# Modulation rows from natural weight rows on VectorE, most of them made during later stages

## The reference

```python
c_act = jax.nn.silu(c)
for layer in range(DEPTH):                                  # 2
    mod = c_act @ ada_w[layer] + ada_b[layer]               # 1024 x 6144, 24 MB a layer
    sh1, sc1, g1, sh2, sc2, g2 = jnp.split(mod, 6, axis=-1)
    h = modulate(rmsnorm(x, norm_mix[layer]), sh1, sc1)     # h * (1 + sc) + sh
    y = retention_mixer(...) if layer == 0 else sgu_mixer(...)
    x = x + g1 * y
    h = modulate(rmsnorm(x, norm_ffn[layer]), sh2, sc2)
    x = x + g2 * peer_ffn(h, ...)                           # 128 experts per token
```

## Time and profile before

| | us |
|---|---|
| median of three runs | 2549.06 |
| profiled execution | 2548.47 |
| its span, first to last instruction | 2546.6 |
| PE busy | 2118.2 (83%) |
| VectorE busy | 1592.1 (63%) |
| ScalarE busy | 1092.5 (43%) |
| POOL busy | 592.9 (23%) |
| DMA | 763.12 MB, 300 GB/s over the span |

### The profile page before, as it was taken

The page is one execution under the profiler, slowest core; times in us unless marked ns, Lnnn a source line. Parts: engine busy times, 40 slices in busy tenths (PEclk is TensorE's granted clock), DMA queues, the critical chain, the costliest instruction groups (busy, mean ns, idle before and its releaser), DMA issues. The chain is left out here.

```text
span 2546.6 us, 24726 instructions
## 1 busy us (share of the span) xinstructions
PE 2118.2 (83%) x8508; PEld 1354.2 (53%) x8508; DVE 1592.1 (63%) x2934; ACT 1092.5 (43%) x2137; POOL 592.9 (23%) x547
## 2 busy tenths in 40 slices
PE   6789997978877878859978787888887887978998
PEld 5669866532222222237967553443332226867996
DVE  6777455776667666534774767767676654555553
ACT  5554433444443444324433444344444343434442
POOL 0000001444444434300000344444344430300000
PEclk9999998999999999979998998999999998889999
DMA  8876535999999999945535899999999994323553
GB/s 310 301 283 234 193 115 178 418 419 421 421 422 421 421 421 422 421 129 179 177 106 173 324 417 376 420 418 419 412 418 421 421 419 130 118 91 116 165 183 132
DMA packets 195327, 763.12 MB, mean 300 GB/s; under 512 B 24545, under 2 KB 26625, under 8 KB 128769
## 3 DMA queue, kind: packets, MB, share of 16 engines
q0 software_dynamic: 75216, 545.88, 51.8%
q1 hardware_dynamic: 105218, 207.75, 23.9%
q10 hardware_dynamic: 14768, 7.92, 1.1%
HBM read 760.41 MB, written 1.10 MB: 299 GB/s over the span
## 5 line engine op out<-in xcount | busy, mean ns | idle before, releaser
L651 PE MATMUL pair<-uv,p_diag 128*128 128x512 f32 x1360 | 668.3, 626 | 160.0 <-ACT p_diag L1623 155.8
L916 DVE TENSOR_TENSOR ring_low<-ring,ring_high 128x2048 fp32r<-128x2048 f32 x196 | 446.1, 2289 | 272.5 <-ACT ring_high L1489 268.4
L1167 DVE CUSTOM_DVE_ANT_0 uv<-uv,p_h 128x1024 f32<-128x1024 f32 x340 | 416.3, 1224 | 302.3 <-DMA uv<-in_peer_uv,p_idx 298.3
L413 POOL DMA_INDIRECT uv<-in_peer_uv,p_idx x340 | 377.5, 1110 | 878.0 <-PE pair L651 466.7
L651 PEld LDWEIGHTS pair<-uv,p_diag 128*128 128x128 f32 x1360 | 245.7, 194 | 559.1 <-ACT p_diag L1623 321.1
L1489 ACT ACTIVATE ring_high<-ring 128x2048 fp32r<-128x2048 f32 x196 | 372.6, 1911 | 321.0 <-DMA ring<-in_ada_w 69.9
L1617 ACT ACTIVATE p_act<-p_dot 128x1 f32<-128x1 f32 x512 | 103.0, 201 | 622.5 <-DVE p_dot L1167 620.9
L522 PE MATMUL pair<-hT_high,ring_high 128*128 128x256 f32 x1056 | 309.5, 293 | 4.6 <-DVE hT_low L926 3.8
L522 PE MATMUL pair<-hT_low,ring_high 128*128 128x256 f32 x1056 | 303.6, 288 | 0.0
L522 PE MATMUL pair<-hT_high,ring_low 128*128 128x256 f32 x1056 | 303.4, 287 | 0.0
L651 PE MATMUL pair<-uv_high,p_diag 128*128 128x512 f32 x464 | 230.9, 630 | 49.8 <-ACT p_diag L1623 48.5
(11 more groups left out here) (312 smaller groups left out, 2739.1 us busy)
## 6 DMA issues: line engine op xcount, KB each, us to landing
ring<-in_ada_w SPq DMA_DIRECT2D x48, 1024.0 KB, 5.2
ring<-in_ret_w_in SPq DMA_DIRECT2D x24, 1024.0 KB, 5.1
ring<-in_sgu_w_in SPq DMA_DIRECT2D x24, 1024.0 KB, 5.2
ring<-in_peer_w_query SPq DMA_DIRECT2D x16, 1024.0 KB, 5.0
ring<-in_w_up SPq DMA_DIRECT2D x16, 1024.0 KB, 5.4
ring<-in_w_down SPq DMA_DIRECT2D x16, 1024.0 KB, 5.1
ring<-in_sgu_w_out SPq DMA_DIRECT2D x12, 1024.0 KB, 5.1
ring<-in_w_in SPq DMA_DIRECT2D x12, 1024.0 KB, 5.1
```

What stands on the lines that cost most here:

```text
L413: nc.gpsimd.indirect_dma_start(uv_rows[SLOT[l][s]].rearrange("p a d -> p (a d)"), None, experts, bass.IndirectOffsetOnAxis(ap=p_idx[:, k:k ...
L651: mm = nc.tensor.matmul(acc[:, half, :], p_diag[:, n % DIAGS, :], v[:, half * 512:(half + 1) * 512], start=(k == 0), stop=(k == PICKS - 1))
L916: did(V.tensor_tensor(ring_low[:, i % R], ring[:, i % R], ring_high[:, high_at[i]].bitcast(F32), ALU.subtract), w_low, i + 1)
L1167: V.tensor_tensor_reduce(out=u, in0=u, in1=p_h[:, s // PICKS, :], scale=1.0, scalar=0.0, op0=ALU.mult, op1=ALU.add, accum_out=p_dot[:, n % ...
```

## The change

The twelve rows are made another way. A tile of `ada_w` is now 128 rows by 1024 columns of one row's part, 0.5 MB in runs of 4 KB. VectorE adds it, scaled by silu(c) of that partition, to the tile before; after eight tiles the sum over partitions is left, and PE takes it with two fp32 products by a matrix of ones, which also spreads it over all partitions. The first tile is added to a tile of zeros that has the bias in partition 0. Scale rows are then completed by VectorE with (1 + row) x gain (`scale_row`), the others are copied by ScalarE (`take_mod`).

Rows are numbered in the order of `MODS`. Rows 0 and 1 are made at the start from sixteen buffers loaded by SyncE. Rows 2 to 7 are made during retention, rows 8 to 11 during the gating mixer; their tiles are loaded by POOL. `STAGED` gives the buffers: four for rows 2 to 6, three for row 7 and for rows 8 to 11. A tile is loaded once the addition after its buffer's last tile is done, or, where that tile was the last of its row, once PE has summed the row. `lows_and_adas(first, counts)` puts so many additions behind each low half.

The first norm and the retention product follow the first two rows; the 48 blocks of `ada_w` leave the ring. The constants by feature are packed on the host in one array `cols` loaded at the start; the other constants go from ScalarE's queue to POOL's. The position weights come turned from the host, and their sum is made by PE within the experts of layer 0. The keys of layer 0 are loaded at the end of retention.

```diff
+MODS = [(0, 1), (0, 0), (1, 0), (1, 1), (0, 2), (0, 3), (0, 4), (0, 5), (1, 2), (1, 3), (1, 4), (1, 5)]
+STAGED = ([[("arena", 8192 + 1024 * i) for i in range(8)], [("arena", 16384 + 1024 * i) for i in range(6)] + [("arena", 2048), ("arena", 3072)]]
+          + 5 * [[("arena", 20480), ("arena", 21504), ("mod", 4), ("mod", 5)]] + [[("arena", 20480), ("arena", 21504), ("mod", 5)]]
+          + 4 * [[("arena", 22528), ("arena", 23552), ("mod", 5)]])
...
+    for v, allowed in enumerate(STAGED):
+        free = [a for a in sorted(allowed, key=lambda a: held.get(a, -1))]
+        for k in range(KD):
+            place.append(free[k % len(free)])
+            before.append(held.get(place[-1]))
+            held[place[-1]] = v * KD + k
...
+        def load_ada(eng, j):
+            (l, part), k, old = MODS[j // KD], j % KD, ADA_BEFORE[j]
+            if old is not None and old % KD == KD - 1:
+                eng.wait_ge(small_ready, SMALL[("mod", old // KD, 1)] + 1)
+            elif old is not None:
+                eng.wait_ge(ada_used, old + 2)
+            eng.dma_start(ada_rows[ADA_AT[j]], w["ada_w"][l, k * P:(k + 1) * P, part * D:(part + 1) * D]).then_inc(ada_landed[j][0], 16)
...
+            sp.dma_start(col[:], w["cols"]).then_inc(c_in, 16)
+            for j in range(KD):
+                load_ada(sp, j)
+            sp.dma_start(x[:], w["x"][0].rearrange("(t p) d -> p t d", p=P)).then_inc(x_in, 16)
+            for j in range(KD, 2 * KD):
+                load_ada(sp, j)
...
+            load_gain_and_bias(0)
+            load_gain_and_bias(1)
+            modulation_rows(range(2, 8))
             gathers(0)
+            pool.wait_ge(x_ready, NORM[2] + 1)
...
+            modulation_rows(range(8, 12))
...
+            def sum_mod(v):
+                pe.wait_ge(ada_used, (v + 1) * KD)
+                rows = ada_rows[ADA_AT[(v + 1) * KD - 1]]
+                for half in range(2):
+                    name = ("mod", v, half)
+                    open_small(name)
+                    nc.tensor.matmul(small_of(name)[:, :], ones[:], rows[:, half * 512:(half + 1) * 512],
+                                     start=True, stop=True).then_inc(small_ready, 1)
...
                 for c in range(4, 12):
+                    if c in (6, 8, 10):
+                        sum_mod(c // 2 - 1)
                     rows_product(("ret_in", c), ("ret_in",), c, hT, KD)
+                sum_mod(5)
...
-                rows_product(("ret_out", 1), ("ret_out",), 1, r_ygT, 16)
+                rows_product(("ret_out", 1), ("ret_out",), 1, r_ygT, 16, lambda kb: sum_mod(6 + kb // 2) if kb % 2 == 0 else None)
...
                 for c in range(6):
+                    if c == 4:
+                        sum_mod(8)
                     rows_product(("sgu_v", c), ("sgu_v",), 6 + c, hT, KD, parts_of_hT(2))
...
+                sum_mod(9)
                 for c in range(6):
+                    if c == 3:
+                        sum_mod(10)
                     columns_product(("sgu_u", c), ("sgu_u",), c, hT)
...
+                    if kb == 1:
+                        sum_mod(11)
...
+            def adas(count):
+                for j in range(ada_done[0], ada_done[0] + count):
+                    v, k = divmod(j, KD)
+                    rows = ada_rows[ADA_AT[j]]
+                    dve.wait_ge(*ada_landed[j])
+                    if k == 0:
+                        dve.wait_ge(bias_in, 16 * (v + 1))
+                    if j:
+                        dve.wait_ge(ada_used, j)
+                    did(V.scalar_tensor_tensor(out=rows, in0=rows, scalar=col[:, k:k + 1], in1=ada_rows[ADA_AT[j - 1]] if k else bias_row,
+                                               op0=ALU.mult, op1=ALU.add), ada_used, j + 1)
...
+            def lows_and_adas(first, counts):
+                for n, count in enumerate(counts):
+                    lows(first + n)
+                    adas(count)
...
+                    if c == 8:
+                        scale_row(3)
+                    lows_and_adas(2 * c + 2, (0, 0) if c == 0 else (1, 1) if c < 4 else (2, 2))
...
+                lows_and_adas(first + 1, (2, 2, 2, 2, 2))
...
-                    lows(block_after(("sgu_v",), 6 + c))
+                    lows_and_adas(first_block_of[("sgu_v", 6 + c)] + 2, (1, 2) if c else (2, 2))
...
-                act.dma_start(s_ws, w["sgu_w_s"][0].rearrange("g i j -> i g j")).then_inc(sgu_in, 16)
-                act.dma_start(s_vbias, bc(w["sgu_b_in"][0:1, HALF:2 * HALF], [P, HALF])).then_inc(sgu_in, 16)
-                act.dma_start(s_bs.rearrange("p g i -> p (g i)"), bc(w["sgu_b_s"].rearrange("a g i -> a (g i)"), [P, GROUPS * P])).then_inc(sgu_in, 16)
...
```

More of the change, by code:

```diff
@@ L68, in matrices @@
 def matrices(w):
-    out = [(("ada", l), w["ada_w"][l], 8, range(12)) for l in range(2)]
-    out += [(("ret_in",), w["ret_w_in"][0], 8, range(12)), (("ret_out",), w["ret_w_out"][0], 16, range(2)),
+    out = [(("ret_in",), w["ret_w_in"][0], 8, range(12)), (("ret_out",), w["ret_w_out"][0], 16, range(2)),
             (("query", 0), w["peer_w_query"][0], 8, range(4)),
@@ L130, in turned, with mods @@
         return [("hT", n, t, g) for t in range(TT) for g in range(2)]
-    out = turned(0) + [("ret_s", h) for h in range(RET_HEADS)] + [("ygT", b) for b in range(8)]
+    def mods(*vs):
+        return [("mod", v, half) for v in vs for half in range(2)]
+    out = mods(0, 1) + turned(0) + mods(2, 3, 4, 5) + [("ret_s", h) for h in range(RET_HEADS)] + [("ygT", b) for b in range(8)] + mods(6, 7)
     for l in range(2):
@@ L137, in small_in_order @@
         if l == 0:
-            out += turned(2) + [("wsT", b) for b in range(2)] + [("ws_sum", b) for b in range(2)]
-            out += [("mixed", b) for b in range(CU // 2)]
+            out += [("ws_sum", b) for b in range(2)] + turned(2) + mods(8, 9, 10)
+            out += [("mixed", b) for b in range(6)] + mods(11) + [("mixed", b) for b in range(6, CU // 2)]
     out += turned(5) + [("attT", 0)]
@@ L639, in peer @@
                     t, h = divmod(i, PEER_HEADS)
+                    if l == 0 and i == WS_UNIT:
+                        pe.wait_ge(ws_zero, 1)
+                        for b in range(2):
+                            name = ("ws_sum", b)
+                            open_small(name)
+                            nc.tensor.matmul(small_of(name)[:, :], ones[:], s_wsT[:, 4 * b:4 * b + 4, :].rearrange("p g i -> p (g i)"),
+                                             start=True, stop=True).then_inc(small_ready, 1)
                     name = ("peer", l, t)
@@ L873, in mlp @@
                     rows_product(("down", c), ("down",), c, f_a, 32, lambda kb: pe.wait_ge(a_low, kb + 1))
[L876 to L892 removed]
             pe.wait_ge(ones_ready, 2)
+            sum_mod(0)
+            sum_mod(1)
+            pe.wait_ge(cst_in, 16)
+            turn_rows(0, r_h)
             retention()
@@ L954, in norm @@
                 settle()
+                if shift_mod is not None:
+                    wait_mod(dve, shift_mod)
                 for t in range(TT):
@@ L1185, in peer @@
                 for i in range(UNITS):
+                    if l == 0 and i == WS_UNIT - 1:
+                        dve.wait_ge(ws_in, 16)
+                        did(V.memset(s_wsT[CHUNK:P, :, 0:CHUNK], 0.0), ws_zero, 1)
                     for k in range(TOPK):
@@ L1251, in sgu @@
                 settle()
[L1252 removed]
+                lows_and_adas(first_block_of[("sgu_u", 2)] + 2, (1, 1))
                 for t in range(TT):
@@ L1524, in columns, with take_mod @@
                 return t.rearrange("p (a b) t -> p a (b t)", b=2)
+            def take_mod(v):
+                for half in range(2):
+                    name = ("mod", v, half)
+                    take_small(name, mod_of(v)[:, half * 512:(half + 1) * 512], small_of(name)[:, :])
             def retention():
-                load_keys(0)
                 for c in range(4):
@@ L1604, in peer @@
                 for i in range(UNITS):
+                    if l == 0 and i == WS_UNIT + 1:
+                        for b in range(2):
+                            take_small(("ws_sum", b), s_wsum[:, 4 * b:4 * b + 4, :].rearrange("p g i -> p (g i)"), small_of(("ws_sum", b))[:, :])
                     if l == 1 and i in (5, 7, 9, 11):
```

293 lines of the change are left out of this document (133 added, 160 removed).

## The result

The changed kernel takes 2473.4 us (median of 4 runs, 2469.2 to 2477.3) against 2550.2 for the kernel before, measured beside it: ratio 0.970, 95% interval 0.967 to 0.973, so 76.8 us less. I had said 2464, in a range from 2425 to 2500.

A forecast was written before the change was run, and what follows sets the result against it. PE bounds retention and gating products, DMA the first stage and experts. Terms -141.3 + 22.5 + 12 + 18.6 + 1.3 + 7.9 - 5.4 = -84.4 took 2548.5 to 2464 us; 8-in-10 range 2425 to 2500, own range 2440 to 2480.

The forecast's parts named there:

- Start: Before retention: only two rows remain to be made, so PE starts at 47 us, -141.3 us.
- Retention product: Retention product: four row sums 6.9, three stops 10, clock 4.2 and 1.4, together +22.5 us.
- Heads: Behind the retention product: head 0's scores wait for row 5's sum, a tile landing and additions, +12 us.
- Output product with what follows: Output product of retention: additions ahead of lows, a 9.6 us stop, row 7's sum and clock, +18.6 us.
- Experts and third norm's reciprocal: Layer 0 experts +1.3 us; the third norm's reciprocal no longer waits for ScalarE's DMA issues, -18.1 us.
- Gating stage behind it: Gating stage: additions, sums and clock 33.3 us on; reciprocal and weight detour 25.4 off, +7.9 in all.
- One sign of the list: First gating product: chunks of 12 to 14 us would show the forecast right.
- Later norms: Later norms: reciprocals find the root 2.3 and 3.1 us sooner, -5.4 us.
- Rival (a): All stages with additions: tiles arrive early wherever VectorE asks, so waits are hidden; 2401 us, chance 0.13.
- Rival (b): Tile loads: landing of 6 us as ring and POOL share, 12 in retention, 10 in gating; 2486 us, chance 0.20.
- Rival (c): All exposed waits: landings beyond 9.3 us make the kernel slower than before, about 2670 at 15.8; chance 0.03.
- the 2443 us worked out from the page: Some 13 exposed landings: by the skill page's 3.2 us each would be 1.6 shorter, giving about 2443 us.

The follow-up runs named there:

- more buffers: Changed kernel with rows 3 to 7 staged in 7, 7, 6, 5 and 4 buffers instead of 4, 4, 4, 4 and 3: 2452.3 us.
- The constants alone: Kernel before with only the constants' new loading and the turned position weights summed during the experts, modulation vectors as before: 2519.6 us.
- the fastest version: Changed kernel with more buffers for rows 3 to 11, later row 11 sum, reordered retention additions, two gating additions per chunk behind the bias addition: 2407.4 us.
- the two other runs with the same second product: Changed kernel with more buffers for rows 3 to 7, 2452.3 us; changed kernel with row 11's sum moved to the second half of the gating output, 2467.2 us.
- the run without reloads: Changed kernel with only the first tile into each buffer transferred for rows 2 to 11, all additions and sums kept: 2429.1 us.
- the narrow tiles: Changed kernel with every tile transfer of rows 2 to 11 but the first into each buffer moving 128 of 1024 columns: 2454.2 us.
- the low halves first: Changed kernel with VectorE making all low halves of a chunk before the chunk's additions, instead of alternating: 2476.8 us.

## Why the prediction was right, step by step

1. Start: PE at 46.91 for 47 said, -141.4 for -141.3. That close is in part luck: the sixteenth tile landed at 32.6 for the 34 said, and what stands behind it took 14.3 for 13.
2. Retention product: up to PE's sum of row 5 at 202.37 it took 155.5, +21.2 for +22.5. The prediction counts the sum of row 5 twice, among the product's four and again in the heads' 12.6; without it the product was to cost +20.8. The three stops are 10.1 us for 10, in the places said. A sum holds the product up by some 1.7, as said. The clock: the same 780 instructions were busy 144.55 us in after and 140.59 with more buffers, 4.0 for stops of 10.1, where I charged 4.2.
3. Heads: the first head's scores (215.51) come 13.1 after the product for 1.6 before, +11.6 for +12.
4. Output product with what follows: 97.4 from there to the second norm for 76.0, +21.4 for +18.6. The large stop was 9.96 for 9.6; the stop at its first low grew from 4.96 to 6.45 us, 1.5 for 1.6; what the other 2.8 us are stays open. Steps 2 to 4 together: +54.2 for +53.1.
5. Experts and third norm's reciprocal: -16.5 for -16.8.
6. Gating stage behind it: **the term that was mis-sized**. Third to fourth norm changed by +34.6 where the sum had +23.7 (33.3 on; 7.3 and the fourth norm's 2.3 off). The constants alone show that the saving is whole, so the cost was: 43.8 for 33.3. In the first product 20.9 for 16.4, in the second 14.3 for 9.1, behind them 8.6 for 3.8; 4 for the clock was charged apart. The stops themselves were sized right: against the constants alone PE stands idle 11.5 us more in the first product (13 said) and 7.8 in the second (7.4 said). What was too small is two things. The clock: in the two products the same work keeps PE busy 80.5 and 75.6 us in after, at a granted clock of 0.87 and 0.94, and 74.5 and 71.2 in the fastest version, at 0.94 and 1.00. That is 10.4 us behind the stops where I charged 4; some 2 of it are of this one execution, since the two other runs with the same second product had PE busy 73.4 and 73.2. And the stop at the sum of row 11: its two calls need the two small accumulators that mixing has just filled, and it is 5.6 of the last 8.6. The prediction counts three sums in this stage and the kernel makes four; neither this sum nor its wait is in any term. One sign of the list failed here too: the chunks of the first product took 13.5 to 21.0 us, 15.7 in the mean, for the 12 to 14 said.
7. Later norms: -3.5 behind the fourth norm, for -3.1.

The sum said -84.4 and the profiled execution shows -72.6; 10.9 of these 11.8 us are step 6.

Rival (a) fell with the run without reloads, by 28 us: even tiles that are there don't hide the additions. Rival (b) wanted landings of 6 us and 2486. Measured are 5.6 in retention and 5.1 in the gating stage in the median, for the 4.8 charged, so the landing lies between the forecast and (b), as the time does. Its 10 us for the gating stage are near the 10.9 that came, but by another cause (clock and row 11's sum); of its 12 in retention 1.1 came. That landings have a price the narrow tiles show: in the gating stage 3.1 us for 5.1, and 13.4 us won. Its premise, that ring and tiles together are at the engines' limit in the product, isn't what the window with more buffers shows: 305 GB/s at a share of 0.85, and no stop. Rival (c) presumes that a slower landing lengthens every wait. In the fastest version tiles land in 6.2 and 7.0 us in the median, and PE has no stop above 1 us in the retention product or the two gating products.

The Trainium skill ("DMA: Bandwidth & Descriptors", section on one DMA by the gpsimd path) gives 3.2 us for such a tile as an estimate, and 2.15 for one of 64 KB. The runs show 5.1 to 5.9 beside the ring and 2.8 to 3.1. The measurement decides; the 2443 us worked out from the page would have been 30 too low.

## What to carry to other kernels

When work is moved beside a busy stage, draw the chain from the release of a buffer to the instruction that queues behind its transfer: release, issue, landing, use, next in the queue. If that chain is longer than the cover, neither spare bandwidth nor spare time of the engine helps, and another order of the instructions behind it only moves the stop, as with the low halves first; what helps is a buffer that is free a round earlier, and memory that is dead or not yet written is where to look for it. Then put what releases another engine ahead of work that nobody waits for.

## What the runs showed of the hardware that I had not expected

Most of a tile's landing doesn't go with its bytes: 64 KB (128 rows of 512 bytes) took 2.8 to 3.1 us and 512 KB (128 rows of 4 KB) 5.1 to 5.9 beside the same ring. Transfers that were issued earlier, into more buffers, took longer each (ring blocks 8.5 for 6.5 us, tiles 6.3 and 7.0 for 5.1 and 5.9) and the kernel is 57 us faster: the median landing says nothing until one sees who waits for it. And a stop of PE costs more than itself: the 312 or 313 instructions of the first gating product were busy 80.5 us at a mean granted clock of 0.87 with three stops of nearly 4 us in it, and 74.5 at 0.94 without one.
